# Mixer order, ring slots, piece order and final norm of a two-block transformer kernel

## The reference

```
# block 1
h = rmsnorm(x, g_mix); b_gate, c_gate, x_in, u, v = split(h @ w_in)          # 5 x 512
y_conv = b_gate * conv3(c_gate * x_in)
y_sgu  = gelu(u) * (spatial mix of layernorm(gelu(v)) per 128 tokens + b_spatial)
x += concat(y_conv, y_sgu) @ w_out
x += moe(rmsnorm(x, g_ffn))      # 4 groups x 8 experts, top group, top 2 in it
x += sigmoid(rmsnorm(x, g_ple) @ w_ple_gate) * (p @ w_ple_proj)
x  = rmsnorm(x, g_final)
# block 2
h = rmsnorm(x, pre)                                       # h @ w_in: 9 x 512
conv_out = silu(layernorm(conv31(glu(conv_in)))) @ w_cb + b
att_out  = stick_breaking_attention(q, k, v) @ w_ab      # log_sigmoid, cumsum, 8 heads
x += rmsnorm((sigmoid(g_conv)*conv_out + sigmoid(g_att)*att_out) @ w_out, post)
x += rmsnorm((silu(gate) * up) @ w_down, ffn_post)        # gate, up = rmsnorm(x, ffn_pre) @ w_up
```

## Time and profile before

| | us |
|---|---|
| three runs | 988.94, 989.81, 992.14 |
| median | 989.81 |
| the profiled execution | 990.13 |
| its span | 988.4 |

### The profile page before, as it was taken

How to read it: one execution, slowest core, us unless ns; L and a number is a source line. 1 busy time by engine, 2 the same in 40 slices (tenths; PEclk the granted TensorE clock), 3 DMA queues, 4 the chain that set the end, 5 groups by cost and what they waited for, 6 DMA issues and landing times.

```text
span 988.4 us, 14242 instructions
## 1 busy us (share of the span) xinstructions
PE 946.4 (96%) x5926; PEld 670.2 (68%) x5926; DVE 497.4 (50%) x866; ACT 330.3 (33%) x527; POOL 36.1 (4%) x39
## 2 busy tenths in 40 slices
PE   6999999999999899999899899999999899999997
PEld 6997734444434444444344689978989899999885
DVE  6595612222222223222122776979898667676632
ACT  5823210101011010101001657555566555544531
POOL 1000000000000000000000000222310000000000
PEclk9999999999999999999999999999999999999999
DMA  8956999999999999999999942532433424555301
GB/s 324 406 233 260 424 407 427 420 430 432 429 430 431 426 431 430 431 430 431 431 425 419 432 189 115 212 129 96 161 133 124 170 107 180 189 201 200 128 1 42
DMA packets 28981, 289.45 MB, mean 293 GB/s; under 512 B 3056, under 2 KB 6384, under 8 KB 12400
## 3 DMA queue, kind: packets, MB, share of 16 engines
q1 hardware_dynamic: 28192, 286.91, 70.9%
q10 hardware_dynamic: 720, 1.57, 0.4%
HBM read 287.43 MB, written 1.05 MB: 292 GB/s over the span
## 4 chain that ended last, share of the span: by engine, by line
PE 87%; DVE 7%; ACT 3%; issue 2%; DMA 1%; SPq 0%; DVEq 0%; ACTq 0%
PE ps L282 86%; DVE wl L278 2%; DVE arena L1531 1%; ACT wh L271 1%; DMA arena<-in_xT 1%; PE ps L1045 1%; DVE arena L589 0%; ACT arena L1835 0%; DVE arena L1737 0%; ACT arena L1838 0%; DVE arena L378 0%; PE ps L2017 0%; ACT in_h L660 0%; DVE arena L1439 0%; DVE arena L584 0%
## 5 line engine op out<-in xcount | busy, mean ns | idle before, releaser
L282 PE MATMUL ps<-ring,arena 128*64 128x512 f32 x1216 | 340.1, 599 | 7.0 <-issue 6.7
L282 PEld LDWEIGHTS ps<-ring,arena 128*64 128x64 f32 x1216 | 109.7, 138 | 166.9 <-issue 164.6
L278 DVE TENSOR_TENSOR wl<-ring,wh 128x1024 fp32r<-128x1024 f32 x150 | 180.2, 1232 | 59.6 <-ACT wh L271 59.4
L271 ACT ACTIVATE wh<-ring 128x1024 fp32r<-128x1024 f32 x150 | 151.0, 1049 | 38.5 <-PE ps L282 28.2
L282 PE MATMUL ps<-arena 128*64 128x512 f32 (+3 forms) x416 | 161.4, 538 | 0.7 <-DVE arena L584 0.5
L1150 DVE SCALAR_TENSOR_TENSOR arena<-ps,arena 128x512 f32<-128x512 f32 x16 | 12.0, 750 | 205.7 <-PE ps L282 205.7
L282 PE MATMUL ps<-up_h,wh 128*128 128x256 f32 x352 | 87.0, 285 | 3.9 <-ACT up_h L1937 3.9
L282 PEld LDWEIGHTS ps<-arena 128*64 128x64 f32 (+1 forms) x416 | 53.2, 141 | 47.0 <-issue 41.2
L282 PE MATMUL ps<-up_l,wh 128*128 128x256 f32 x352 | 83.0, 283 | 0.0
L1220 ACT ACTIVATE y_h<-ps 128x512 fp32r<-128x512 f32 x32 | 19.1, 597 | 158.1 <-PE ps L282 158.1
L282 PEld LDWEIGHTS ps<-up_h,wh 128*128 128x128 f32 x352 | 67.1, 191 | 4.3 <-issue 4.3
(11 more groups left out here) (263 smaller groups left out, 1508.0 us busy)
## 6 DMA issues: line engine op xcount, KB each, us to landing
ring<-in_moe SPq DMA_DIRECT2D x69, 2048.0 KB, 24.2
arena<-in_moe SPq DMA_DIRECT2D x17, 2048.0 KB, 25.9
ring<-in_w_in SPq DMA_DIRECT2D x12, 2048.0 KB, 10.5
ring<-in_w_up SPq DMA_DIRECT2D x11, 2048.0 KB, 7.7
ring<-in_moe SPq DMA_DIRECT2D x20, 512.0 KB, 15.0
ring<-in_w_dn SPq DMA_DIRECT2D x5, 2048.0 KB, 7.7
ring<-in_w_out SPq DMA_DIRECT2D x4, 2048.0 KB, 15.9
arena<-in_moe SPq DMA_DIRECT2D x12, 512.0 KB, 13.1
```

What stands on the lines that cost most here:

```text
L271: e.activation(wh(i), raw_piece(i), ACT.Copy).then_inc(*hi.up(i))
L278: e.tensor_tensor(wl(i), raw_piece(i), wh(i), SUB).then_inc(*lo.up(i))
L282: return e.matmul(o, l, r, start=first, stop=final, skip_group_check=True)
```

## The change

- The tile `pproj` leaves the stream; `w_pp` is loaded into an area `PPW` of the arena behind tile d0. The slots of the expert tiles shift by one, and the special slot of the last one goes.
- Mixer: two runs of `split_hi` move (one behind the gelu of the first rows, one ahead of the squares); the scaling of v stands behind the second gate product; the spatial products stand between the second and third part of tile 4; the two first gated rows and their low parts are formed ahead of the spatial result, all low parts come in the order 0, 1, 4, 5, 6, 7, 2, 3, and out1 reads them so.
- Experts and gate: one piece of pgate is rounded ahead of the last y copies, low pieces no longer stand between the last additions. `XN` goes; the rounding of block 2's rows scales by `gpre` = g_final * pre2. The first four pieces of in2 are made one per round (j = 1 to 4).
- in2 and attention: `softplus_dve(0)` stands ahead of the last k product; `r4` and `x4` move to `out2_dve`, with g_final in the product; 12 taps take their place, and the rounds of attention do three taps.
- End: the last six k of x = 1 are done for one bank, then for the other; the product by the gain is formed ahead of the reciprocal, and scale and residual are one operation.

```diff
@@ -24,3 +24,3 @@
 RING = 8
-N0 = 8
+N0 = 7
 N1 = N0 + 96
...
@@ -28,3 +28,3 @@
 
-SLOTS = ([0, 1, 2, 3, 8, 0, 1, 2], [3, 8, 0, 1, 9, 5, 7, 4, 6, 2], [2, 3, 0, 1])
+SLOTS = ([0, 1, 2, 3, 8, 0, 1], [2, 3, 8, 0, 9, 1, 5, 7, 4, 6], [2, 3, 0, 1])
 SLOT = 4096
...
@@ -50,3 +50,3 @@
 def stream():
-    out = [("in1", i) for i in range(5)] + [("out1", i) for i in range(2)] + [("pproj", 0)]
+    out = [("in1", i) for i in range(5)] + [("out1", i) for i in range(2)]
     out += moe_order()
...
@@ -400,2 +397,3 @@
         PT = A(o + 4864, 2, 256)
+        PPW = A(o + 2560, 2, 1024)
         SM = A(o + 5384, 720)
...
@@ -424,5 +422,5 @@
         mixed = sig("mixed", range(4))
-        mix_h = xg_h.then([4, 5, 6, 7, 0, 1, 2, 3])
+        mix_h = xg_h.then([0, 1, 4, 5, 6, 7, 2, 3])
         bgate = sig("bgate", range(4))
-        mix = xg.then([4, 5, 6, 7, 0, 1, 2, 3])
+        mix = xg.then([0, 1, 4, 5, 6, 7, 2, 3])
         wrg = sig("wrg", range(8))
...
@@ -578,3 +575,10 @@
                 e.tensor_tensor(CR[:, j, :], ps[CB[j]][:, 0:256], R2B, M).then_inc(*cgate.up(j))
-                split_lo(e, j + 15)
+                split_lo(e, 15 + j)
+                if j == 1:
+                    e.wait_ge(*vsq.at(1))
+                    e.tensor_scalar(VV, VV, 1.0 / 512, None, M).then_inc(*vvar.up(0))
+                    recip(e, "vv", VV)
+                    e.wait_ge(*recips.at("vv"))
+                    for i in range(2):
+                        e.tensor_scalar(VG[:, i, :], VG[:, i, :], VV[:, i:i + 1], None, M).then_inc(*vn.up(i))
             for j in range(4):
...
@@ -592,3 +596,17 @@
                 e.tensor_tensor(CR[:, j, :], CR[:, j, :], R1B, M).then_inc(*conv.up(j))
-                split_lo(e, j + 19)
+                split_lo(e, j + 20)
+            split_lo(e, 24)
+            def gated(j):
+                e.wait_ge(*proj.at("in1", 4, j))
+                e.tensor_tensor(CR[:, j, :], ps[CB[j]][:, 0:256], CR[:, j, :], M).then_inc(*bgate.up(j))
+
+            def rest(c):
+                src = CR[:, c, :] if c < 4 else Z[:, c - 4, 2:258]
+                e.wait_ge(*mix_h.at(c))
+                e.tensor_tensor(MIXL[:, c, :], src, MIXH[:, c, :], SUB).then_inc(*mix.up(c))
+
+            gated(0)
+            gated(1)
+            rest(0)
+            rest(1)
             e.wait_ge(l_bb, 32)
...
@@ -606,11 +624,9 @@
                 e.tensor_tensor(mj, mj, UG[:, j, :], M).then_inc(*mixed.up(j))
-            for j in range(4):
-                e.wait_ge(*mix_h.at(4 + j))
-                e.tensor_tensor(MIXL[:, 4 + j, :], Z[:, j, 2:258], MIXH[:, 4 + j, :], SUB).then_inc(*mix.up(4 + j))
-            for j in range(4):
-                e.wait_ge(*proj.at("in1", 4, j))
-                e.tensor_tensor(CR[:, j, :], ps[CB[j]][:, 0:256], CR[:, j, :], M).then_inc(*bgate.up(j))
-                e.wait_ge(*mix_h.at(j))
-                e.tensor_tensor(MIXL[:, j, :], CR[:, j, :], MIXH[:, j, :], SUB).then_inc(*mix.up(j))
-                split_lo(e, j + 23)
+            gated(2)
+            for c in (4, 5, 6, 7, 2):
+                rest(c)
+            split_lo(e, 25)
+            gated(3)
+            split_lo(e, 26)
+            rest(3)
 
...
@@ -666,3 +683,3 @@
             root(e, "r1", R1B, ps[2][:, 0:256])
-            split_hi(e, 9)
+            split_hi(e, 8)
             e.wait_ge(l_xk, 16)
...
@@ -684,2 +701,3 @@
                              accum_out=VS[:, i:i + 1]).then_inc(*gelu_v.up(i))
+            split_hi(e, 16)
             for i in range(2):
...
@@ -691,10 +709,11 @@
             root(e, "vv", VV, VV)
-            split_hi(e, 22)
-            for j in range(4):
-                e.wait_ge(*mixed.at(j))
-                e.activation(MIXH[:, 4 + j, :], Z[:, j, 2:258], ACT.Copy).then_inc(*mix_h.up(4 + j))
-            for j in range(4):
-                e.wait_ge(*bgate.at(j))
-                e.activation(MIXH[:, j, :], CR[:, j, :], ACT.Copy).then_inc(*mix_h.up(j))
-                split_hi(e, j + 23)
+            split_hi(e, 24)
+            for c in (0, 1, 4, 5, 6, 7, 2, 3):
+                if c < 4:
+                    e.wait_ge(*bgate.at(c))
+                    e.activation(MIXH[:, c, :], CR[:, c, :], ACT.Copy).then_inc(*mix_h.up(c))
+                else:
+                    e.wait_ge(*mixed.at(c - 4))
+                    e.activation(MIXH[:, c, :], Z[:, c - 4, 2:258], ACT.Copy).then_inc(*mix_h.up(c))
+                split_hi(e, {0: 25, 1: 26, 2: 27}.get(c, 0))
 
...
@@ -1193,5 +1211,3 @@
                     rest(q, 1)
-                    split_lo(e, FIRST + 1)
                     add(q, 0)
-            split_lo(e, FIRST + 2)
             add(NP - 1, 1)
...
@@ -1213,2 +1229,4 @@
                 e.activation(HT.rearrange("p a b -> p (a b)"), ps[4][:, :], ACT.Copy).then_inc(*b4.up(q))
+                if q == NP - 1:
+                    split_hi(e, FIRST + 1)
                 for n in range(2):
...
@@ -1401,4 +1418,6 @@
             def parts(j):
-                e.wait_ge(*xn.at(j))
-                e.activation(H5H[:, j, :], XN[:, j, :], ACT.Copy, scale=vcol("pre2", j)).then_inc(*h5_h.up(j))
+                e.wait_ge(*x3.at(j))
+                if j == 0:
+                    e.wait_ge(*made.at("gpre"))
+                e.activation(H5H[:, j, :], XT[:, j, :], ACT.Copy, scale=gpre[:, j:j + 1]).then_inc(*h5_h.up(j))
                 e.wait_ge(*sq3.at(j))
...
@@ -1415,2 +1434,3 @@
                     e.preload_act_table_set("sigmoid_and_others")
+                split_hi(e, FIRST + 8 + min(j, 4))
                 if j >= 1:
...
@@ -1419,3 +1439,2 @@
                     parts(j - 3)
-                split_hi(e, FIRST + (8 if j < 4 else 10 if j == 4 else 12))
             sigmoid(7)
...
@@ -1446,8 +1465,7 @@
                 e.tensor_tensor(XT[:, j, :], XT[:, j, :], TM[:, j % 4, :], ADD).then_inc(*x3.up(j))
-                e.wait_ge(*x3.at(j))
-                e.tensor_scalar(XN[:, j, :], XT[:, j, :], vcol("g_final", j), None, M).then_inc(*xn.up(j))
 
             def parts(j):
+                e.wait_ge(*x3.at(j))
                 e.wait_ge(*h5_h.at(j))
-                e.scalar_tensor_tensor(out=H5L[:, j, :], in0=XN[:, j, :], scalar=vcol("pre2", j), in1=H5H[:, j, :],
+                e.scalar_tensor_tensor(out=H5L[:, j, :], in0=XT[:, j, :], scalar=gpre[:, j:j + 1], in1=H5H[:, j, :],
                                        op0=M, op1=SUB).then_inc(*h5.up(j))
...
@@ -1464,3 +1482,3 @@
                     parts(j - 3)
-                split_lo(e, FIRST + (8 if j < 4 else 10 if j == 4 else 12))
+                split_lo(e, FIRST + (8, 8, 9, 10, 12, 12, 12, 12)[j])
             scale(7)
...
@@ -1697,2 +1715,4 @@
             for j in range(4):
+                if j == 3:
+                    softplus_dve(e, 0)
                 e.wait_ge(*proj.at("in2", 3, j))
...
@@ -1709,8 +1728,4 @@
             split_lo(e, IN2 + 24)
-            recip(e, "r4", RB[:, 1, :])
-            e.wait_ge(*recips.at("r4"))
-            for c in range(8):
-                e.tensor_tensor(XT[:, c, :], XN[:, c, :], RB[:, 1, :], M).then_inc(*x4.up(c))
-                if c == 5:
-                    softplus_dve(e, 2)
+            taps_dve(e, 12)
+            softplus_dve(e, 2)
             taps_dve(e, 6)
...
@@ -1733,4 +1748,2 @@
                 dst, jj = (SGC if n < 2 else SGA), 4 * (n % 2) + j
-                if g == 0:
-                    e.wait_ge(*x4.at(7))
                 e.wait_ge(*proj.at("in2", 5 + n, j))
...
@@ -1750,3 +1763,3 @@
                     softplus_dve(e, 3)
-                taps_dve(e, 4)
+                taps_dve(e, 3)
                 if g in (2, 4, 6, 8):
...
@@ -1942,2 +1955,10 @@
         def out2_dve(e):
+            split_lo(e, OUT2 + 6)
+            recip(e, "r4", R4)
+            e.wait_ge(*recips.at("r4"))
+            for c in range(8):
+                if c == 4:
+                    split_lo(e, OUT2 + 8)
+                e.scalar_tensor_tensor(out=XT[:, c, :], in0=XT[:, c, :], scalar=vcol("g_final", c), in1=R4, op0=M,
+                                       op1=M).then_inc(*x4.up(c))
             split_lo(e, OUT2 + 14)
...
@@ -2087,5 +2109,18 @@
                 part(k, 1)
-            for x in range(2):
+            for k in range(16, 22):
+                part(k, 0)
+
+            for h in range(2):
+                b = ps[2 + h][:, :]
                 for k in range(16, 22):
-                    part(k, x)
+                    i = n_piece[("fdn", k // 4), k % 4]
+                    for v in (WH, WL):
+                        r = v[:, i % 8, h * 512:h * 512 + 512]
+                        z = mm(e, b, FFH[:, k, 128:256], r, False, k == 21 and v is WL)
+                        if v is WH:
+                            mm(e, b, ffl(k)[:, 128:256], r, False, False)
+                    if h:
+                        z.then_inc(*proj.up("fdn", k, 1))
+                    elif k == 21:
+                        z.then_inc(*proj.up("fdn", "half"))
 
...
@@ -2115,4 +2150,8 @@
```

(17 more changed lines are left out.)

58 lines of the change are left out of this document (26 added, 32 removed).

## The result

The changed kernel takes 974.32 us (median of four, 973.18 to 975.34) against 989.38 us for the kernel before in the same comparison: a ratio of 0.9846 (95% interval 0.9826 to 0.9866), 15.1 us less. The prediction had 12.7 us less and 977.1 us; the time lies in its range near the lower end. The profiled execution took 974.7 us with a span of 972.9, 15.5 less than before.

A forecast was written before the change was run, and what follows sets the result against it. PE was taken to set the end nearly everywhere, with the weight stream in the experts, so gains come from PE's idle stretches and the tail. 2.5 + 0.95 + 1.7 + 2.5 + 2.1 + 1.5 + 1.5 = 12.75 us, giving 977.1 (974.0 to 982.5).

The forecast's parts named there:

- Mixer: Mixer: gelu wait of 0.44 us goes and DVE's new order saves waits; PE leaves 2.1 us sooner.
- Stream: Expert weight stream: u4 is issued 2.1 us sooner and lands earlier, moving the whole stream; 2.5 us.
- The extra for an emptier queue: Weight stream: with older tiles done, u4 lands up to 1.2 us sooner beyond the mixer's 2.1.
- The rival that the stream moves by ten us: Weight stream gains the older tiles' full ten us and PE's data waits of 3.63 + 3.48 go; 970.4 us, chance 0.05.
- the one that it doesn't move: Weight stream: u4's slot comes free no sooner, or older transfers still lie ahead; 979.6 us, chance 0.2.
- Gate piece and clock: Gate start: one piece rounded earlier shortens PE's wait by 0.95 us; the half-clock stretch behind it goes, 1.7 us.
- in2's first pieces: Start of in2: pieces made one per gate round instead of in pairs, so PE's wait at 588.30 goes; 2.5 us.
- Softplus: Attention: softplus of head 0 moved ahead of the fourth k product, so PE's wait at 646.38 goes; 2.1 us.
- The fear for softplus of head 2: Attention: if GpSimd slows the 12 moved taps, PE may wait up to 2 us for softplus of head 2.
- Attention's end: End of attention: three taps per round instead of four let DVE catch up, cutting waits near 726; 1.5 us.
- Output projection: Output projection: r4 and x4 moved here delay nothing PE waits for; 0, at worst a loss of 1.3 us.
- Tail: After the last matmul: one square less, gain product beside the root, two operations instead of four; 1.5 us.

The follow-up runs named there:

- e2: The changed kernel with the old mixer orders on PE, DVE and ACT put back, new ring kept; 978.22 us.
- e4: The kernel before with only the new ring, w_pp taken out of the weight stream's slots; 989.38 us.
- e1: The kernel before, run again unchanged; 989.22 us, ratio 1.0.
- e5: The changed kernel with the piece that was put behind the first gelu moved ahead of ACT's squares again; 976.34 us.
- e3: The changed kernel with w_pp back in the ring and the old slots, new mixer order kept; 973.85 us.
- e6: The changed kernel with the first two pieces of pgate rounded together behind the last y copies again; 975.07 us.
- e7: The changed kernel with the first four pieces of in2 made in pairs again; 977.55 us.
- e9: The changed kernel with r4 and x4 back in in2 instead of the 12 taps, and four taps per attention round; 974.88 us.
- n1: The changed kernel with nine taps instead of six behind softplus of head 2, so the last attention round has none; 972.50 us.

## Why the prediction was right, and where it was off

In the two profiled executions the lead of after over before grows by place as follows, with the prediction's terms for the same stretch beside it:

| up to (its start in before and after) | lead, us | grown by | forecast |
|---|---|---|---|
| first rows of the gate (557.89 and 552.80) | 5.1 | 5.1 | 2.5 + 0.95 |
| first load of in2 (588.30 and 578.77) | 9.5 | 4.4 | 1.7 + 2.5 |
| softplus of head 0 (646.38 and 634.20) | 12.2 | 2.7 | 2.1 |
| mean over the convolution (729.66 and 716.92) | 12.7 | 0.6 | 1.5 |
| first load of fup (787.39 and 774.03) | 13.4 | 0.6 | 0 |
| first square behind the matmuls (981.06 and 967.46) | 13.6 | 0.2 | 0 |
| end of the span (988.4 and 972.9) | 15.5 | 1.9 | 1.5 |

The total came out 2.8 us below the forecast. Part of its nearness is luck: the mixer gave more than forecast and attention less, and the two misses go opposite ways.

- **What bounds the kernel.** Right: with no matmul removed, everything came out of PE's gaps, its stretches at half clock and the tail.
- **Mixer, 2.1 us forecast, 3.9 by e2 and 4.35 in the profiles.** The step that failed is "the piece that is put behind the gelu takes ACT some 1.0 us, more than the gap". The gap of 0.44 in the earlier trace rows was taken as the price of that wait. It was what was left of it after PE had started late and lost 1.7 us to the lower clock at 13. Without that stretch the wait is 1.05, 1.94 and 2.27 us (e4, e2, e1), and 4.10 in the profile of e5, where ACT waits longest for the tile. The piece costs not its 1.0 us but ACT's wait for a landing, 4.1 to 5.6 us over these five profiles, a row that was in the trace and was not read. The other term, DVE's order, was 1.65 and comes out at 1.4 to 2.0. Of the 4.35 us at the last mix_l, 0.7 are PE's earlier start; the rest is the half-clock stretch of that one profile of before, its wait of 0.44 and the order.
- **Stream, 2.5 us forecast for a mixer gain of 2.1.** Half right. That u4's slot ties the whole stream to the end of the first down projection holds: its issue keeps 60.7 us behind the last mix_l, and all between mixer and gate moves one for one (table under e2). The extra for an emptier queue doesn't: the ring is worth nothing (e3, e4). The rival that the stream moves by ten us and the one that it doesn't move both fall.
- **Gate piece and clock, 0.95 + 1.7.** The gap shrank by 0.98 (2.42 to 1.44); in eight other profiles with this piece it is 1.1, but there PE's loads of the last down projection wait 1.8 to 2.5 us instead of 1.46. In the profiles that have a gap of over 2 us in the gate or ahead of in2 (before, e1, e4, e6, e7) there is one stretch of 3.4 us at half clock between 550 and 590; in the other nine there is none. So the 1.7 us are real, but they belong to the two gaps together: after one has been closed the other can still have it. Undone alone the two edits cost 0.75 and 3.2, together 4.0; forecast were 0.95 + 1.7 + 2.5 = 5.2.
- **in2's first pieces, 2.5.** Right in mechanism; the gap is 2.16 with the pairs alone, and 3.2 in the time with the clock.
- **Softplus, 2.1.** Right: 2.13 us of gap, 2.6 in the time. The fear for softplus of head 2 was empty, since GpSimd did not run beside most of the 12 taps.
- **Attention's end, 1.5.** Wrong: 0.6 by e9. One gap was seen as DVE being behind by one tap a round. DVE was behind by its whole rest, and the last of it, three taps, holds the next step of PE. The wait moved by one place, and n1 shows it: with those three taps done sooner the gap is gone. The prediction had asked what is late next for softplus and did not ask it here.
- **Output projection, 0.** No gap came in, as forecast: the wait ahead of fup is 4.27 in both.
- **Tail, 1.5.** 1.9 in the trace and 1.7 in the time.

Undone one by one, the parts come to 3.9 (mixer) + 0.75 + 3.2 + 2.6 + 0.6 + 1.7 = 12.8 us of the 15.1 (the ring, -0.5, is not told from zero). Each has an uncertainty of about 1 us or more, so 2.3 are within it; the parts not undone alone (the low pieces between the last additions, the norm sums one tile sooner) may hold some, and the 0.6 us by which the lead grows between the convolution and fup have no cause shown. That stays open.

## What to carry to other kernels

A wait is worth what it would be with everything ahead of it on time; when a profile has one accident ahead of a wait (here a slow clock), look at the releasing engine's own timeline and at what that engine stood still for. A piece moved past a wait for a transfer moves all that is queued behind it, so count the wait and not the piece. When a gap at the end of a stage is closed, list what else the next step needs from the same engine: the cheapest fix was to use an idle stretch of DVE 60 us earlier.

## What the runs showed of the hardware

- The granted clock fell for 3.4 us behind gaps in PE's loads of 2.2 to 2.6 us in the gate and ahead of in2, but not at the same one each time: at 559.4 in one profile of before, at 586.5 in the next, behind the gap of 2.56 us there, with the gap of 2.43 at 557 passing without. In the mixer it fell behind the gaps of 2.27 (e1) and 4.10 us (e5), and not behind 1.94 (e2). The run of before again had this window at the start of in2:

```profile
586.50:589.80 3.30, 3.30 (x18) 3.30 (x17) 3.16 (x10) 1.96 (x6) 0.00 (x0) 0.50 0.88 293
```

- The same transfer of 2 MB, u4, took between 7.8 and 9.7 us from issue to landing in six executions: 9.0, 8.1 and 9.7 with the old ring, 7.8, 8.3 and 9.3 with the new one. So a difference of 1 us in one profile says nothing on the queue.
- Twelve taps on DVE took 4.83 us where GpSimd was idle for most of them (0.40 each), and four took 3.60 in the earlier trace rows where it ran (0.90 each).
